# Loads moved under the last project tile, and block sums stored from GpSimd's queue

## The reference

```
h   = (x * (1 + m1) + m0) @ w_in                      # 1824 columns: latents, keys, values, queries, conv
A   : kv = rms(c_kv) @ w_ukv ; q = rms(c_q) @ w_uq ; rotary ; attention, 6 heads
B   : grouped-query attention, 6 heads, 2 key heads, rms on q and k, 2-D rotary
C   : cb * conv3(cc * ch)
x1  = layer_norm(ALPHA * x + m2 * (concat(A, B, C) @ w_o))
out = layer_norm(ALPHA * x1 + m5 * (relu((x1 * (1 + m4) + m3) @ w1) ** 2 @ w2))
```

## Time and profile before

| what | value |
|---|---|
| median of 3 executions | 3241.82 us (3240.65 to 3245.42) |
| the profiled execution | 3244.43 us, span 3242.6 us, mean clock 0.975 |
| TensorE matmul busy | 3073.8 us (95%), 13713 |
| TensorE weight load busy | 2271.0 us (70%) |
| VectorE busy | 2335.3 us (72%), 3190 |
| ScalarE busy | 1345.5 us (41%), 1915 |
| GpSimd busy | 1395.1 us (43%), 826 |
| DMA | 515.49 MB, mean 159 GB/s |

### The profile page before, as it was taken

How to read it: one execution, slowest core, us unless ns; L and a number is a source line. 1 busy time by engine, 2 the same in 40 slices (tenths; PEclk the granted TensorE clock), 3 DMA queues, 4 the chain that set the end, 5 groups by cost and what they waited for, 6 DMA issues and landing times. The chain is left out here.

```text
span 3242.6 us, 38639 instructions
## 1 busy us (share of the span) xinstructions
PE 3073.8 (95%) x13713; PEld 2271.0 (70%) x13713; DVE 2335.3 (72%) x3190; ACT 1345.5 (41%) x1915; POOL 1395.1 (43%) x826
## 2 busy tenths in 40 slices
PE   6999958999999999999999997999999999999995
PEld 2888845566565656656566776888788888888784
DVE  4355446777777877777766888777678758887887
ACT  3223222434344344444443335655555544433441
POOL 1233301576775766765662225333333234314421
PEclk8999977999999999999999998999999999999998
DMA  6222378224332223330215678435644487877873
GB/s 238 65 83 78 91 222 276 66 61 102 88 82 72 61 62 88 68 81 14 55 33 188 234 263 312 155 143 191 253 160 156 146 321 281 304 263 288 292 274 149
DMA packets 235706, 515.49 MB, mean 159 GB/s; under 512 B 26705, under 2 KB 101841, under 8 KB 223313
## 3 DMA queue, kind: packets, MB, share of 16 engines
q1 hardware_dynamic: 229296, 489.17, 45.7%
q10 hardware_dynamic: 6240, 24.12, 2.1%
HBM read 356.64 MB, written 156.57 MB: 158 GB/s over the span
## 5 line engine op out<-in xcount | busy, mean ns | idle before, releaser
L1095 DVE TENSOR_REDUCE h_mpart<-a_mx 128x1 f32<-128x512 f32 x920 | 569.0, 636 | 264.9 <-PE a_mx L1188 256.3
L1032 POOL TENSOR_TENSOR a_acc_p<-a_acc_p,a_pf 128x1024 f32<-128x1024 f32 x240 | 581.4, 2422 | 212.2 <-ACT a_pf L1075 186.3
L1075 ACT ACTIVATE a_pf<-o_y 128x1024 f32<-128x1024 f32 x432 | 442.5, 1024 | 481.7 <-PE o_y L1214 481.3
L2189 PE MATMUL f_bank<-slots,f_wx 128*128 128x512 f32 x2304 | 573.3, 391 | 8.2 <-DMA slots<-s_uc 8.2
L2197 PE MATMUL f_bank<-slots 128*128 128x512 f32 x2128 | 507.1, 391 | 12.8 <-DVE slots L1974 9.7
L2189 PEld LDWEIGHTS f_bank<-slots,f_wx 128*128 128x128 f32 x2304 | 434.2, 189 | 100.7 <-DMA slots<-s_uc 10.2
L2197 PEld LDWEIGHTS f_bank<-slots 128*128 128x128 f32 x2128 | 399.8, 188 | 99.8 <-DVE slots L1974 13.5
L2144 POOL TENSOR_TENSOR f_y<-f_y,raw_rows 128x1024 f32<-128x1024 f32 x80 | 218.9, 2737 | 405.5 <-DMA raw_rows<-in_w 405.5
L2135 POOL TENSOR_TENSOR f_work<-raw_rows 128x512 f32<-128x512 f32 x160 | 220.7, 1381 | 380.1 <-DVE f_wx L1967 367.0
L1988 DVE TENSOR_TENSOR f_work<-f_work,f_bank 128x512 f32<-128x512 f32 x256 | 174.5, 682 | 134.5 <-ACT f_work L1866 123.7
L500 PE MATMUL p_main<-win_hi,u_hi 128*128 128x512 f32 (+2 forms) x528 | 198.2, 375 | 20.5 <-POOL u_lo L443 19.8
(11 more groups left out here) (275 smaller groups left out, 5408.1 us busy)
## 6 DMA issues: line engine op xcount, KB each, us to landing
raw_rows<-s_hx SPq DMA_DIRECT2D x112, 512.0 KB, 4.1
f_y<-in_w SPq DMA_DIRECT2D x112, 512.0 KB, 5.3
raw_rows<-in_w SPq DMA_DIRECT2D x80, 512.0 KB, 5.7
raw_rows<-in_w SPq DMA_DIRECT2D x32, 1024.0 KB, 4.9
s_hx<-stream SPq DMA_DIRECT2D x128, 256.0 KB, 2.7
s_hx<-f_work SPq DMA_DIRECT2D x96, 256.0 KB, 2.2
a_wa<-in_w_ada SPq DMA_DIRECT2D x8, 2048.0 KB, 8.8
slots<-s_uc ACTq DMA_DIRECT2D x10, 1024.0 KB, 15.3
```

What stands on the lines that cost most here:

```text
L1032: nc.gpsimd.tensor_tensor(acc[:, :], left[:, :], pf[(b * KT + kt) % NPF][:, :], ALU.add).then_inc(added_p, 1)
L1075: nc.scalar.activation(pf[n % NPF][:, :], sc[n % 2][:, :], ACT.Exp, scale=SCALES[0 if is_mla(b) else 1]).then_inc(exped, 1)
L1095: nc.vector.reduce_max(mpart[b % 2][:, s, k:k + 1], mx[c % 2][:, 0:CHUNKS[k][1]], AX.X).then_inc(mx_read, 1)
L2189: mm = nc.tensor.matmul(by_pair(bank[:, m % 8, :]), w[:, k], x[s][:, :, k * P:(k + 1) * P], start=(k == 0 and j == 0), stop=(k == 3 and j ...
```

## The change

It has two parts. First, the seven loads of latents and tables that the expansion's first block needs are issued by SyncE in the project stage, between the stores of the last tile but one and those of the last; they now wait for all matmuls of the stage (`bank_done`) and for the stores of all tiles but the last two. For this the memory of the next stages is opened (`open_expansion`) where the project stage's instructions begin, at the addresses of the weights. In the expansion SyncE now begins with the loads of block 1 and the remaining key latents, ahead of the store of the context's keys. Second, in the mix stage the stores of the block sums leave SyncE's order and stand in GpSimd's: the store of position `pos - 2` ahead of the sum of position `pos`, the last two at the pair's end. SyncE keeps the mix loads and the row stores.

```diff
@@ -179,7 +179,8 @@
 def stage_project(nc, g, a):
 
     with ExitStack() as ctx:
-        sb = lambda n, s, d=F32: ctx.enter_context(nc.sbuf_tensor(n, s, d))
+        mem = ctx.enter_context(ExitStack())
+        sb = lambda n, s, d=F32: mem.enter_context(nc.sbuf_tensor(n, s, d))
         ps = lambda n, s: ctx.enter_context(nc.psum_tensor(n, s, F32))
         sem = lambda n: early_semaphore(nc, g, "p_" + n)
         w_hi, w_lo = g.w_hi, g.w_lo
@@ -218,6 +219,8 @@
         turned, hi_out, lo_out, stored = sem("turned"), sem("hi_out"), sem("lo_out"), sem("stored")
         v_set = sem("v_set")
         w_up_in, w_up_hi, w_up_lo = [sem(f"w_up_in{i}") for i in range(len(EXPANSION))], sem("w_up_hi"), sem("w_up_lo")
+        mem.close()
+        open_expansion(nc, g)
         block = ctx.enter_context(nc.Block())
 
         STORES_C, STORES_X = 7, 13
@@ -313,6 +316,12 @@
                     for done, (at, w, _, _) in zip(w_up_in, EXPANSION):
                         sp.dma_start(at, w).then_inc(done, 16)
                 step(0, c)
+            sp.wait_ge(bank_done, banks_before(CT + TT))
+            sp.wait_ge(stored, stores_before(CT + TT - 2))
+            load_ckv(sp, g, 0, slice(0, CTX))
+            load_cq(sp, g, 0)
+            load_ckv(sp, g, 1, slice(CTX, CTX + QB))
+            sp.dma_start(g.e_cs[0][:, :, :], a["cs_rope"][:, :, 0:QB]).then_inc(g.cs_in[0], 16)
             store(CT + TT - 1, True)
             sp.wait_ge(stored, stores_before(CT + TT))
 
@@ -522,16 +531,44 @@
             schedule(pe, split, work, out, in_halves=True)
 
 
+def open_expansion(nc, g):
+
+    g.w_in.close()
+    g.raw_rows = g.ctx.enter_context(nc.sbuf_tensor("raw_rows", [P, 4, D], F32))
+    g.rows = [g.raw_rows[:, i, :] for i in range(4)]
+    g.raw = g.raw_rows[:, :, :].rearrange("p (q r) n -> p q (r n)", q=2).rearrange("p q (k f) -> p q k f", k=KD)
...
+    g.expansion = ExitStack()
+    sb = lambda n, s, d=F32R: g.expansion.enter_context(nc.sbuf_tensor("e_" + n, s, d))
+    g.ckv_hi, g.ckv_lo = sb("ckv_hi", [P, KEYS]), sb("ckv_lo", [P, KEYS])
+    g.cq_hi, g.cq_lo = ([sb(f"cq_{part}{i}", [P, 2, QB]) for i in range(NQB)] for part in ("hi", "lo"))
+    g.e_cs = [sb(f"cs{i}", [6 * 16, 2, QB], F32) for i in range(NQB)]
+    sem = lambda n: g.expansion.enter_context(nc.semaphore("e_" + n))
+    g.ckv_in = [sem(f"ckv_in{i}") for i in range(3)]
+    g.cq_in, g.cs_in = [sem(f"cq_in{i}") for i in range(NQB)], [sem(f"cs_in{i}") for i in range(NQB)]
+
+
+def load_ckv(eng, g, part, cols):
+    for half, t in enumerate((g.ckv_hi, g.ckv_lo)):
+        eng.dma_start(t[:, cols].bitcast(F32), g.ckv[half][:, cols]).then_inc(g.ckv_in[part], 16)
+
+
+def load_cq(eng, g, b):
+    for half, t in enumerate((g.cq_hi, g.cq_lo)):
+        eng.dma_start(t[b][:, :, :].bitcast(F32), g.cq[half][:, :, b * QB:(b + 1) * QB].rearrange("c p t -> p c t")).then_inc(g.cq_in[b], 16)
+
+
 def stage_expand(nc, g, a):
 
     with ExitStack() as ctx:
         sb = lambda n, s, d=F32: ctx.enter_context(nc.sbuf_tensor("e_" + n, s, d))
         ps = lambda n, s: ctx.enter_context(nc.psum_tensor("e_" + n, s, F32))
         sem = lambda n: ctx.enter_context(nc.semaphore("e_" + n))
-        ckv_hi, ckv_lo = sb("ckv_hi", [P, KEYS], F32R), sb("ckv_lo", [P, KEYS], F32R)
-        cq_hi = [sb(f"cq_hi{i}", [P, 2, QB], F32R) for i in range(NQB)]
-        cq_lo = [sb(f"cq_lo{i}", [P, 2, QB], F32R) for i in range(NQB)]
-        cs = [sb(f"cs{i}", [6 * 16, 2, QB]) for i in range(NQB)]
+        ctx.enter_context(g.expansion)
+        ckv_hi, ckv_lo, cq_hi, cq_lo, cs = g.ckv_hi, g.ckv_lo, g.cq_hi, g.cq_lo, g.e_cs
         uq_hi, uq_lo, ukv_hi, ukv_lo = g.uq_hi, g.uq_lo, g.ukv_hi, g.ukv_lo
         st_hi, st_lo = sb("st_hi", [P, 2, 3, QB], F32R), sb("st_lo", [P, 2, 3, QB], F32R)
         rt, ro = sb("rt", [6 * 16, 4, QB]), sb("ro", [6 * 16, 2, QB])
...
@@ -568,27 +604,17 @@
 
         @block.sync
         def _(sp):
-            def load_ckv(part, cols):
-                for half, t in enumerate((ckv_hi, ckv_lo)):
-                    sp.dma_start(raw(t[:, cols]), g.ckv[half][:, cols]).then_inc(ckv_in[part], 16)
-
             def load(b):
-                tok = slice(b * QB, (b + 1) * QB)
-                for half, t in enumerate((cq_hi, cq_lo)):
-                    sp.dma_start(raw(t[b][:, :, :]), g.cq[half][:, :, tok].rearrange("c p t -> p c t")).then_inc(cq_in[b], 16)
-                if b == 0:
-                    load_ckv(1, slice(CTX, CTX + QB))
-                sp.dma_start(cs[b][:, :, :], a["cs_rope"][:, :, tok]).then_inc(cs_in[b], 16)
+                load_cq(sp, g, b)
+                sp.dma_start(cs[b][:, :, :], a["cs_rope"][:, :, b * QB:(b + 1) * QB]).then_inc(cs_in[b], 16)
 
             def store_set(kind, items, dst, tok):
                 sp.wait_ge(lo_set, items)
                 for half, t in enumerate((st_hi, st_lo)):
                     sp.dma_start(dst[half][:, tok].rearrange("(c p) t -> p c t", p=P), raw(t[:, kind, :, 0:tok.stop - tok.start])).then_inc(st_stored[kind], 16)
-            load_ckv(0, slice(0, CTX))
-            load(0)
+            load(1)
+            load_ckv(sp, g, 2, slice(CTX + QB, KEYS))
             store_set(1, 3, g.kn, slice(0, CTX))
-            load(1)
-            load_ckv(2, slice(CTX + QB, KEYS))
             for b in range(NQB):
                 store_set(0, items_before(b) + 3, g.qn, slice(b * QB, (b + 1) * QB))
                 store_set(1, items_before(b) + 6, g.kn, slice(CTX + b * QB, CTX + (b + 1) * QB))
@@ -1391,22 +1417,19 @@
             for q in range(2):
                 sp.dma_start(g.raw[:, q], a["w1"][q]).then_inc(mlp_in, 16)
 
-            def store_sums(p):
-                for pos in range(NP):
-                    use = ring_use(p, pos)
-                    if use is None:
-                        continue
-                    sp.wait_ge(lo_set, NP * p + pos + 1)
-                    for part, at in enumerate((ring_hi, ring_lo)):
-                        sp.dma_start(g.uc[p // 4, pos, part][:, p % 4, :], raw(at[use % RING])).then_inc(uc_stored[use % RING], 16)
-            for s, t in enumerate(TILE):
-                if s + 2 < TT:
-                    sp.wait_ge(y_done, s + 1)
-                    load_mix(sp, g, s + 2)
-                if s and s % 2 == 0:
-                    store_sums(s // 2 - 1)
+            def load_tile(s):
+                if s < TT:
+                    sp.wait_ge(y_done, s - 1)
+                    load_mix(sp, g, s)
+
+            def store_row(s):
                 sp.wait_ge(x1_set, s + 1)
-                sp.dma_start(g.x1[t * P:(t + 1) * P, :], x1[s % 2]).then_inc(x1_stored[s % 2], 16)
+                sp.dma_start(g.x1[TILE[s] * P:(TILE[s] + 1) * P, :], x1[s % 2]).then_inc(x1_stored[s % 2], 16)
+            for p in range(PAIRS + 1):
+                load_tile(2 * p + 2)
+                store_row(2 * p)
+                load_tile(2 * p + 3)
+                store_row(2 * p + 1)
             sp.wait_ge(cols_in, 16)
             sp.wait_ge(mlp_in, 32)
             uses = ring_use(PAIRS - 1, NP - 1) + 1
@@ -1518,14 +1541,28 @@
 
         @block.gpsimd
         def _(pool):
+            def store_sum(p, pos):
+                use = ring_use(p, pos)
+                if use is None:
+                    return
+                pool.wait_ge(lo_set, NP * p + pos + 1)
+                for part, at in enumerate((ring_hi, ring_lo)):
+                    pool.dma_start(g.uc[p // 4, pos, part][:, p % 4, :], raw(at[use % RING])).then_inc(uc_stored[use % RING], 16)
+
             def sums(p):
-                for pos in SUMS["right"]:
+                for pos in range(NP):
+                    if pos >= 2:
+                        store_sum(p, pos - 2)
+                    if pos not in SUMS["right"]:
+                        continue
                     first, second, sign = right_parts(u, ORDER[pos])
                     k = sums_before(p, pos)
                     pool.wait_ge(u_set, 2 * p + 2)
                     if k >= SUM_RING:
                         pool.wait_ge(lo_set, summed_lows(k - SUM_RING))
                     nc.gpsimd.tensor_tensor(total[k % SUM_RING], first, second, plus(sign)).then_inc(sum_set, 1)
+                for pos in (NP - 2, NP - 1):
+                    store_sum(p, pos)
             pool.wait_ge(rows_in, 32)
             for s in range(TT):
                 if s and (s - 1) % 2:
@@ -2275,19 +2312,10 @@
     with ExitStack() as ctx:
         g = make_shared(nc, ctx, a)
         g.ctx, g.banks = ctx, ctx.enter_context(ExitStack())
-        w_in = ctx.enter_context(ExitStack())
-        g.w_hi, g.w_lo = (w_in.enter_context(nc.sbuf_tensor(f"win_{part}", [P, KD, NCOL], F32R)) for part in ("hi", "lo"))
-        g.xt = [w_in.enter_context(nc.sbuf_tensor(f"xt{i}", [P, KD, P], F32)) for i in range(2)]
+        g.w_in = ctx.enter_context(ExitStack())
+        g.w_hi, g.w_lo = (g.w_in.enter_context(nc.sbuf_tensor(f"win_{part}", [P, KD, NCOL], F32R)) for part in ("hi", "lo"))
```

(21 more changed lines are left out.)

## The result

| | us |
|---|---|
| kernel before, 4 executions | 3243.03 median (3240.65 to 3245.42) |
| changed kernel, 4 executions | 3269.47 median (3265.92 to 3271.21) |
| ratio | 1.0083, 95% interval 1.0069 to 1.0098 |
| profiled execution of the change | 3265.92, span 3264.3, mean clock 0.970 |

The change costs 26.4 us by the medians. The forecast of 3271.1 is within 2 us, but the traces show that this is luck: its two terms were wrong by 5.6 and 15.5 us in opposite directions, and what they leave over is made up by 7 us that the forecast had no term for.

A forecast was written before the change was run, and what follows sets the result against it. Transfers were taken to bind the expansion until 531 us, VectorE's serial order the output projection. Stores +34.3 and latents -5.0 gave +29.3 on 3241.8, so 3271.1 us; range 3243.7 to 3285.5, widened to 3240 to 3291.

The forecast's parts named there:

- its two terms: Block sums' stores on GpSimd's queue in the mix stage, +34.3 us; latents loaded earlier for the expansion, -5.0 us.
- d = 1.0 us: Mix stage: time GpSimd takes to issue one block sum store, taken as 1.0 us between bounds 0.44 and 1.30.
- the formula: Mix stage cost of the moved stores: 3 (10 d - 2.6) + 4 (4 d - 0.4) - 2.35 = 46 d - 11.75.
- The stores' landing does not bind: Mix stage, late pairs: position 0's store is out 2 d after the low, its buffer's next high comes 4 d + 1.3 after.
- 3 x (10 d - 2.6): Mix stage: cost of the three late pairs, all seven positions stored, ten issues on the path of each.
- VectorE's -2.35: Mix stage: VectorE's 2.35 us wait at 1829.28 goes once mix loads no longer stand behind the sums' stores.
- 4 x (4 x 0.548 - 0.4): Mix stage: cost of the four early pairs, 4 d - 0.4 each, here with the measured issue time as d.
- nearer the lower: Expansion: gain from early latents taken as 5.0 us, between 4.3 (TensorE's waiting gone) and 6.6 (2.23 MB less to move).
- The rival of the eaten gain: Expansion: keys' store queued behind the loads that now go first eats the latents' 5.0 us, so 3276; chance 0.15.
- An issue next to free, and TensorE's waits as the bound: Mix stage: issues cost next to nothing, 10.6 us of mix waits and the latents' 5.0 go, 3226; chance 0.10.
- An issue like the other queues': Mix stage: GpSimd issues in 0.32 to 0.44 us, +3.0 to +8.5 less 5.0, 3240 to 3245; chance 0.13.
- The port fight: Mix stage: each pair of GpSimd stores first waits out a VectorE low of 0.69, adding 16 us, 3287; chance 0.12.

The follow-up runs named there:

- loads_held: The full change, but SyncE holds each odd tile's mix loads until the lows of the pair before are done; ratio 1.0064 to the kernel before.
- keys_store_first: Kernel before with only the latents' loads moved, and the context keys' store issued ahead of block 1's queries and remaining latents; 3239.32 us, ratio 0.9987.
- start_reordered: Kernel before with latents' loads moved, keys' store between block 1's queries and remaining latents, first heads' loads after three query copies; 3233.62 against 3240.37 us, ratio 0.9974.
- start_again: Repeat of start_reordered, run beside heads_later and old_heads_later; ratio 0.9973 to the kernel before.
- heads_later: Kernel before with latents' loads moved, keys' store behind them as in the change, and first heads' loads issued after ScalarE's first three query copies; ratio 0.9979.
- old_heads_later: Kernel before with one edit, the first heads' loads issued after the first three query copies, no part of the change; ratio 0.9998.

## Why the prediction was right, and where it was wrong

**The bounds.** VectorE's serial order does set the pace of the mix stage: the issues counted on the chain low, store, sum, high, low came onto the stage nearly one for one when they were doubled. Freeing TensorE of 9.9 us of waits bought much less, and in one place only: the pair with the 2.35 us wait, 28.55 us long before, became 27.17, while its three early neighbours grew by 2.34 to 2.38; so the relief was worth 3.7 us there. (With the stores on SyncE's queue this pair took 25.0 to 28.2 us in the other six profiles, so that even this gain is not the same in each execution.)

**The price of an issue.** This term failed most. I took d = 1.0 us, nearer to GpSimd's 1.30 of a whole sum than to SyncE's 0.44, and the issues took 0.548 us on average, near that lower bound. With 46 issues on the path this overstated the cost by 46 x 0.452 = 20.8 us. "The work is done by the engine whose row is 1.30" was the bad argument: an issue does not take its time from a pass over the tile, since one of half the rows took 0.52 us too.

**What else the stores cost.** With the measured d the formula gives 46 x 0.548 - 11.75 = +13.5, and the stage shows +18.8. The stage from the row of 1886.91 on, where the late pairs are, grew by 13.1 us (98.03 to the MLP's first product, 84.93 from 1880.34 before), where 3 x (10 d - 2.6) gives 8.6. In the pair shown above the lows took 4.7 us more, where the formula gives 2.9. Of that 1.8, 0.7 is the landing (14.6 against 13.9 with the loads held). The sentence "The stores' landing does not bind" failed: in this order of sums and stores it holds for short landings (`loads_held` has no such wait), and the mix loads that SyncE was now free to issue made some of them 5 to 7 us. Most of the other 1.1 is in sums beside a low: with the loads held three of the four take 1.60 to 1.62 us, where I had counted 1.30 for each, 0.9 in all. The early pairs and VectorE's -2.35 came out near their terms only together: 4 x (4 x 0.548 - 0.4) - 2.35 = 4.8, and the stage up to the row of 1886.91 grew by 5.7 (137.61 us from ln_cols, 131.91 before). Taken singly, an early pair cost 2.35 us, not 1.8, and the relief was 3.7, not 2.35.

**The latents.** The forecast took 5.0 us and had it "nearer the lower" bound because the keys' store would be late next. That mechanism was named, and was one of the rivals; only its size was wrong, since the wait it made was 15.4 us and took everything. I had counted SyncE's queue and overlooked that ScalarE's heads' loads depend on a latent that now comes early. The rival of the eaten gain, at 0.15, is what happened, and the main case of 0.50 was wrong here.

**The sum.** +34.3 was +18.8 and -5.0 was +0.6, together 19.4 and not 29.3. Of the 7.0 us from there to the 26.4 of the medians, 2.1 are in the MLP, which the forecast left out, and 5 lie between the profiled executions and the medians. So the total was met by luck twice over, by errors of opposite sign and by these 7 us; without the error in d the same forecast would have said 3241.8 + 13.5 - 5.0 = 3250.3, same direction and three times too small an effect.

**The rivals.** An issue next to free, and TensorE's waits as the bound: excluded, no issue took less than 0.52 us, and relief of TensorE gave 3.7 us. An issue like the other queues': the row came near it, but the time did not follow, since landing and sums added to it. The port fight: no store issue took more than 0.71 us, so none waited out a low. The Trainium skill's "SBUF — State Buffer", the "DVE blocks DMA" box, speaks of VectorE in a two-port operation, such as a copy of fp32; the lows here are TENSOR_TENSOR, and nothing of the box shows. What shows is the fight between computations that was there before: GpSimd's sums take 1.60 us beside a low and 1.29 without, and of the late pairs' lows two take 1.58 and 1.79 us beside a sum (1903.82 and 1968.74), where the usual is 0.69. "Small, variable" of "DMA: Bandwidth & Descriptors", section "Anatomy of one DMA", did not fit: the issue was steady at 0.52 to 0.56 and, ten to a pair, not small. The same page, section "Issuing engines are not separate DMA queues", says that DMAs from all issuing engines run on the same 16 DMA engines and interleave, so that another queue saves only the issue time. The traces agree at both places: the keys' store lands in 5.4 us before and in 12.9 us with ScalarE's loads issued ahead of it (`keys_store_first`), and GpSimd's stores land in 2.8 us at the median and in up to 6.9 beside a load of SyncE.

**The signs named beforehand.** Held: highs waiting for sums; no wait for mix tiles to speak of; no stall between 423 and 434; queries starting within 4 us of the first keys (3.1). Held in kind but not in size: the odd rows' spacing, 31.4 us in late pairs (34 expected), and in early ones 2.4 more three times and 1.4 less once (3.6 more expected); TensorE idle before its turns, 5.0 and 5.3 us in late pairs (8 or more expected):

```profile
1947.16 1.97 PE L1587 MATMUL o_t_x<-ident,o_r 128*128 128x128 f32 x8 [5.31 <-DVE o_r L1518]
```

Failed: issues near 1 us, and key maxima 5 us earlier.

## What to carry to other kernels

Moving stores to an idle engine's queue moves their issue time too: here 0.54 us each, in program order between computations that others wait for. Count the issues that stand on that engine's path, and put first the computations that need not follow them. Here that order paid clearly only together with the held loads (8.3 of 18.8 us).

A queue that is relieved issues its next loads sooner, and a load moved earlier releases whatever waits for it. Before moving one, list every transfer that is released with it, on all queues, and ask which small store that an engine waits for will then stand behind them. Here holding back 2176 KB that nobody needed yet turned a move worth nothing into 7 us.

Check a sum term by term even when the total is right.

## What was not expected of the hardware

The same 768 KB store of keys landed in 5.4 us with the queue clear, 12.9 beside 2176 KB of another queue, 12.2 behind 2944 KB of its own, and 21.9 behind both. The kernels that hold the heads' loads also moved more from 441 to 525 us: 355 GB/s in `start_reordered`, 354 in `start_again`, 351 in `heads_later` and 343 in `old_heads_later`, against 335 in `keys_store_first`, 332 before and 320 with the change; the row of `start_reordered`:

```profile
441.00:525.00 84.00, 68.01 (x242) 49.98 (x241) 52.76 (x82) 27.16 (x49) 0.00 (x0) 0.83 1.04 355
```

The start became 10 us shorter, more than the upper bound of 6.6 in the forecast, which took the rate as fixed and knew nothing of the heads' loads. Why the rate rose was not tried.

Whether a fourth ring buffer would hide the landings was not tried either. The fastest kernels here are `start_reordered`, 0.26% under the kernel before (0.27% in its repeat), and `heads_later`, 0.21% under it, which the intervals do not tell apart; both store the block sums from SyncE.
